# A DeltaNet mixer that keeps its keys unnormalised, with the z and gate projections merged and the layer norm's sums added over channel groups first

## The reference, cut to what matters

```python
qkv, z, b_logit, a_logit, cf_in = split(h @ w_in)          # 1536, 512, 4, 4, 1024 columns
q, k, v = split(silu(causal_conv4(qkv)))                   # 4 heads of 128
q, k = l2norm(q), l2norm(k)                                # x * rsqrt(sum(x*x) + EPS)
beta = sigmoid(b_logit);  g = -exp(a_log) * softplus(a_logit + dt_bias)
o = gated_delta_rule(q, k, v, g, beta)                     # S_t = e^g S + beta k (v - e^g S^T k)^T
o = rms_norm(o, dn_norm_w) * silu(z)
cf = silu(layer_norm(causal_conv31(glu(cf_in + b))))       # mean and variance over 512 channels
mixed = concat([o, cf]) @ w_out
```

## Time and profile before

| what | value |
|---|---|
| median of 3 runs | 2866.58 us (2862.74 to 2869.66) |
| the profiled execution's own time | 2864.63 us |
| its span, first to last instruction | 2862.8 us |
| mean granted clock of PE | 0.948 |
| PE busy, share of the span | 2533.9 us, 89% |
| DVE busy | 1337.9 us, 47% |
| ACT busy | 818.2 us, 29% |
| POOL busy | 477.5 us, 17% |

### The profile page before, as it was taken

The page is one execution under the profiler, slowest core; times in us unless marked ns, Lnnn a source line. Parts: engine busy times, 40 slices in busy tenths (PEclk is TensorE's granted clock), DMA queues, the critical chain, the costliest instruction groups (busy, mean ns, idle before and its releaser), DMA issues. The chain is left out here.

```text
span 2862.8 us, 48765 instructions
## 1 busy us (share of the span) xinstructions
PE 2533.9 (89%) x18064; PEld 1613.3 (56%) x18065; DVE 1337.9 (47%) x3734; ACT 818.2 (29%) x1760; POOL 477.5 (17%) x735
## 2 busy tenths in 40 slices
PE   6879999999999999999974699999999999999940
PEld 5567777887778877778852343334334343333310
DVE  1468787788887788887863200000000000000037
ACT  1213433343433343433331122222212122221211
POOL 0112221222221222212220210111101010100112
PEclk9889999999999999999976699999999999999975
DMA  9430000000000000000000899999999999999957
GB/s 357 167 121 16 32 24 24 32 32 16 32 17 31 32 22 25 32 17 31 24 24 25 341 376 398 401 387 427 385 398 399 367 427 376 423 420 410 365 230 315
DMA packets 84326, 570.79 MB, mean 199 GB/s; under 512 B 16189, under 2 KB 16573, under 8 KB 56138
## 3 DMA queue, kind: packets, MB, share of 16 engines
q1 hardware_dynamic: 67298, 525.47, 45.6%
q0 software_dynamic: 13824, 33.58, 3.0%
q10 hardware_dynamic: 3048, 9.34, 0.8%
HBM read 534.71 MB, written 50.40 MB: 204 GB/s over the span
## 5 line engine op out<-in xcount | busy, mean ns | idle before, releaser
L364 PE MATMUL pj_ps<-hT,win 128*128 128x128 f32 x5120 | 635.5, 279 | 4.4 <-issue 4.4
L364 PEld LDWEIGHTS pj_ps<-hT,win 128*128 128x128 f32 x5120 | 593.1, 192 | 23.0 <-issue 10.1
L1122 DVE SCALAR_TENSOR_TENSOR cvf<-cfpre,chp,cvf 128x128 f32<-128x128 f32 x1920 | 594.1, 372 | 12.6
L1802 PE MATMUL gate_ps<-longgu,xT 128*64 128x512 f32 x752 | 337.5, 602 | 31.3 <-DMA shortgu<-in_w_gate_dram 28.3
L1819 PE MATMUL y_ps<-longdn,hidT 128*64 128x512 f32 x752 | 331.4, 593 | 20.1 <-ACT hidT L1865 20.1
L1879 DVE TENSOR_TENSOR hid<-hid,up_ps 128x512 f32<-128x512 f32 x47 | 32.3, 688 | 670.4 <-PE up_ps L1802 670.4
L1802 PE MATMUL gate_ps<-shortgu,xT 128*64 128x512 f32 x752 | 337.5, 602 | 0.0
L1819 PE MATMUL y_ps<-shortdn,hidT 128*64 128x512 f32 x752 | 332.8, 595 | 0.0
L1802 PE MATMUL up_ps<-longgu,xT 128*64 128x512 f32 x752 | 330.4, 592 | 0.0
L1802 PE MATMUL up_ps<-shortgu,xT 128*64 128x512 f32 x752 | 330.4, 592 | 0.0
L1883 DVE COPY y<-y_ps 128x512 f32<-128x512 f32 x94 | 65.0, 692 | 381.2 <-PE y_ps L1819 381.2
(11 more groups left out here) (322 smaller groups left out, 3247.7 us busy)
## 6 DMA issues: line engine op xcount, KB each, us to landing
shortgu<-in_w_gate_dram SPq DMA_DIRECT2D x47, 2048.0 KB, 9.4
shortgu<-in_w_up_dram SPq DMA_DIRECT2D x47, 2048.0 KB, 13.7
shortdn<-in_w_down_dram SPq DMA_DIRECT2D x47, 2048.0 KB, 13.2
longgu<-in_w_gate_dram SPq DMA_DIRECT2D x20, 2048.0 KB, 13.4
longgu<-in_w_up_dram SPq DMA_DIRECT2D x20, 2048.0 KB, 18.1
longdn<-in_w_down_dram SPq DMA_DIRECT2D x20, 2048.0 KB, 18.9
wout<-in_w_ada_dram SPq DMA_DIRECT2D x12, 2048.0 KB, 8.7
yy<-y_dram SPq DMA_DIRECT2D x16, 1024.0 KB, 11.9
```

Of the source, the lines that this page charges most:

```text
L364: mm = pe.matmul(pj[bank][:, g % 4, :], t.win[:, k, col + (g % 4) * P:col + (g % 4 + 1) * P], hT[:, k, :], start=(k == 0), stop=(k == KD - 1))
L1122: ins = dve.scalar_tensor_tensor(cvf[:, g, :], src, w, cvf[:, g, :], ALU.mult, ALU.add)
L1802: mm = pe.matmul(out[sides[side], :], xT[:, k, sides[side]], w[:, m * KD + k, :], start=(k == 0), stop=(k == KD - 1))
```

## The change

Five edits go together.

1. The norms of the keys leave the keys. `scores` works on the raw keys (qkvT itself, channel-major), so khat, its transposes on PE and the evacuation of them on ACT disappear. ACT copies the key rows out of b5 (`krow`) and squares that copy. POOL makes rk = rsqrt(ssk1), sqk = ssk1 * rk (the norm), bk = beta * rk and bh = bk * rk; EU is multiplied by bh (in turn i, not at the end of the turn before). v is scaled by the norm (`scaled_values` on DVE, where `khats` was), and `state_values` subtracts in SBUF. The state update's key decay uses the last column of EU.
2. One of the three 4-column products of `decays` goes, and `front_kdb` on DVE.
3. z and the 8 gate columns (520 columns next to each other in w_in) become two products of 260 columns, in banks pj[0] and pj[1], on either side of `state_and_output`. `project_ba` goes. ACT evacuates with two Silu and a copy of 8 columns. z_evac is signalled after the three.
4. The sums of the layer norm over 4 channel groups: POOL adds the groups two and two, then one and one (`channel_sum`, `square_sum`), and PE multiplies one group with the ones matrix where it did four.
5. The query norm is folded in the head norm, so `head_rstd` has two steps where it had five, and POOL raises to a power once less.

```diff
@@ PE
-            def project_z(j, first, last):
+            def project_z(j, part):
-                if first == 0:
-                    pe.wait_ge(k_evac, j + 1)
-                for k in range(first, last):
-                    mm = pe.matmul(pj[0][:].rearrange("p a b -> p (a b)"), hT[:, k, :], t.win[:, k, COL_Z:COL_Z + DNW],
+                pe.wait_ge((k_evac, v_evac)[part], j + 1)
+                for k in range(KD):
+                    mm = pe.matmul(pjf[part][:, 0:ZH], hT[:, k, :], t.win[:, k, COL_Z + part * ZH:COL_Z + (part + 1) * ZH],
                                    start=(k == 0), stop=(k == KD - 1))
-                if last == KD:
+                if part == 1:
                     mm.then_inc(z_ps, 1)
...
-                pe.matmul(m_gate[:, 4:8], t.cst[:, C_LS, :], g4, start=True, stop=True)
-                pe.matmul(m_gate[:, 8:12], t.cst[:, C_ONE, :], g4, start=True, stop=True).then_inc(gates_ps, 1)
+                pe.matmul(m_gate[:, 4:8], t.cst[:, C_ONE, :], g4, start=True, stop=True).then_inc(gates_ps, 1)
...
             def ln_mean(i):
-                pe.wait_ge(cf_tap, CFT * (i + 1))
+                pe.wait_ge(csum_ready, i + 1)
                 pe.wait_ge(ssn_ready, i + 1)
-                for g in range(CFG):
-                    mm = pe.matmul(m_mean, t.cst[:, C_ONE, :], cvf[:, g, :], start=(g == 0), stop=(g == CFG - 1))
-                mm.then_inc(mean_ps, 1)
+                pe.matmul(m_mean, t.cst[:, C_ONE, :], csum, start=True, stop=True).then_inc(mean_ps, 1)
             def ln_var(i):
-                pe.wait_ge(xc_sq, i + 1)
-                for g in range(CFG):
-                    mm = pe.matmul(m_var, lnsq[:, g, :], t.cst[:, C_ONE, 0:1], start=(g == 0), stop=(g == CFG - 1))
-                mm.then_inc(var_ps, 1)
+                pe.wait_ge(vsum_ready, i + 1)
+                pe.matmul(m_var, lnsq[:, 0, :], t.cst[:, C_ONE, 0:1], start=True, stop=True).then_inc(var_ps, 1)
...
             def scores(i):
-                pe.wait_ge(khatT_ready, i + 1)
+                pe.wait_ge(k_copied, i + 1)
...
                 ada_turn(i, 8)
-                pe.wait_ge(khat_ready, i + 1)
-                for h in range(HEADS):
-                    mm = pe.transpose(b5[:, h, :], khat[:, h, :], ident)
-                mm.then_inc(khatT_ps, 1)
+                scores(i)
                 if front:
                     project(j, 4, 5)
-                scores(i)
...
                 if front:
-                    project_z(j, 0, KD // 2)
+                    project_z(j, 0)
                 state_and_output(i)
                 if front:
-                    project_z(j, KD // 2, KD)
-                    project_ba(j)
+                    project_z(j, 1)
@@ ACT
-                act.activation(zn[:], pj[0][:], ACT.Silu).then_inc(z_evac, 1)
+                act.wait_ge(ba_biased, j)
+                znf = zn[:].rearrange("p h c -> p (h c)")
+                act.activation(znf[:, 0:ZH], pjf[0][:, 0:ZH], ACT.Silu)
+                act.activation(znf[:, ZH:DNW], pjf[1][:, 0:DNW - ZH], ACT.Silu)
+                act.copy(bar, pjf[1][:, DNW - ZH:ZH]).then_inc(z_evac, 1)
...
             def key_squares(i):
                 act.wait_ge(kr_ps, i + 1)
+                act.wait_ge(dS_ps, i)
+                act.copy(krow[:], b5[:]).then_inc(k_copied, 1)
+                act.wait_ge(k_copied, i + 1)
                 act.wait_ge(ssk_eps, i)
                 for h in range(HEADS):
-                    ins = act.activation(tmp[:, h, :], b5[:, h, :], ACT.Square, accum_out=ssk[:, h:h + 1])
+                    ins = act.activation(tmp[:, h, :], krow[:, h, :], ACT.Square, accum_out=ssk[:, h:h + 1])
...
-                khat_evac(i)
@@ POOL
+            def key_norms(i):
                 pool.wait_ge(ssk_ready, i + 1)
...
+                pool.tensor_tensor(rk, ssk1, hp[:, 4:8], ALU.pow).then_inc(k_scale, 1)
+            def key_scales(i):
...
+                pool.tensor_tensor(sqk, ssk1, rk, ALU.mult).then_inc(sqk_ready, 1)
+                pool.tensor_tensor(bk, beta, rk, ALU.mult).then_inc(k_scale, 1)
+                pool.wait_ge(k_scale, 3 * i + 2)
+                pool.tensor_tensor(bh, bk, rk, ALU.mult).then_inc(k_scale, 1)
...
+                pool.tensor_tensor(EU[:], EU[:], over_cols(bh, P), ALU.mult).then_inc(EU_ready, 1)
             def key_decay(i):
...
+                pool.tensor_tensor(krow[:], krow[:], over_cols(EU[:, :, P - 1], P), ALU.mult).then_inc(kdec_ready, 1)
+            def channel_sum(i):
+                pool.wait_ge(cf_tap, CFT * (i + 1))
+                pool.wait_ge(qkv_act, i + 1)
+                pool.tensor_tensor(csum2, cvf[:, 0:2, :], cvf[:, 2:4, :], ALU.add).then_inc(csum_half, 1)
+                pool.wait_ge(csum_half, i + 1)
+                pool.tensor_tensor(csum, csum2[:, 0, :], csum2[:, 1, :], ALU.add).then_inc(csum_ready, 1)
+            def square_sum(i):
+                pool.wait_ge(xc_sq, i + 1)
+                pool.tensor_tensor(lnsq[:, 0:2, :], lnsq[:, 0:2, :], lnsq[:, 2:4, :], ALU.add).then_inc(vsum_half, 1)
+                pool.wait_ge(vsum_half, i + 1)
+                pool.tensor_tensor(lnsq[:, 0, :], lnsq[:, 0, :], lnsq[:, 1, :], ALU.add).then_inc(vsum_ready, 1)
...
             def turn(i, before, front, ahead):
                 j = i + 1
+                key_norms(i)
                 if before:
                     rsqrt_row(ss1, v1, rs1, mix_ss, mix_var, mix_rstd, i - 1)
-                keys(i)
+                key_scales(i)
                 if before:
                     rsqrt_row(ss2, v2, rs2, x1_ss, x1_var, x1_rstd, i - 1)
-                key_decay(i)
+                channel_sum(i)
                 mask(i, 0)
                 first_n(i)
                 mask(i, 1)
                 mask(i, 2)
                 state(i)
+                square_sum(i)
                 mask(i, 3)
                 ln_rstd(i)
+                key_decay(i)
@@ DVE
-            def khats(i):
-                dve.wait_ge(rqk_ready, 2 * i + 1)
-                dve.wait_ge(dS_ps, i)
-                dve.tensor_tensor(khat[:], b5, over_cols(rqk[:, 4:8], P), ALU.mult).then_inc(khat_ready, 1)
+            def scaled_values(i):
+                dve.wait_ge(sqk_ready, i + 1)
+                dve.wait_ge(vr_ps, i + 1)
+                dve.wait_ge(oa_ps, i)
+                dve.tensor_tensor(xv[:], b6, over_cols(sqk, P), ALU.mult).then_inc(vs_ready, 1)
...
-                dve.tensor_tensor(xv[:], b6, eS[:], ALU.subtract).then_inc(x_ready, 1)
+                dve.tensor_tensor(xv[:], xv[:], eS[:], ALU.subtract).then_inc(x_ready, 1)
```

More of the change, by code:

```diff
@@ L137, in build_mixer @@
         zn, zg = sb("zn", [P, HEADS, HD]), sb("zg", [P, HEADS, HD])
-        small = sb("small", [P, 96])
+        small = sb("small", [P, 104])
         qkvT = sb("qkvT", [P, QKVG, P])
@@ L155, in build_mixer @@
         P6 = KX
-        ssk, eps_k, ssk1 = ksum[:, 0:4], ksum[:, 4:8], ksum[:, 8:12]
+        ssk, eps_k, ssk1, rk, bk, bh, sqk = (ksum[:, 4 * n:4 * n + 4] for n in range(7))
         lnsq = sq[:, 0:CFG, :]
         lnd = cv[:, 2 * HEADS, :]
+        csum2, csum = cv[:, HEADS:HEADS + 2, :], cv[:, HEADS + 2, :]
         (ss0, rs0, ss1, rs1, ss2, rs2, v0, v1, v2) = (small[:, n:n + 1] for n in range(9))
-        ssn, rqk = small[:, 10:18], small[:, 18:26]
+        ssn = small[:, 10:14]
         bal, en, e8 = small[:, 26:34], small[:, 34:42], small[:, 42:50]
         l4, sp4, g4 = small[:, 50:54], small[:, 54:58], small[:, 58:62]
-        beta, kdb = small[:, 62:66], small[:, 66:70]
-        ex = small[:, 70:82]
+        beta, ex = small[:, 62:66], small[:, 70:78]
         oss, orr = small[:, 82:86], small[:, 86:90]
-        eps_d, eps_hd2 = small[:, 90:91], small[:, 91:95]
+        eps_d = small[:, 90:91]
+        bar = small[:, 96:104]
         hp = sb("half_pow", [P, 8])
-        scr = sb("scr", [P, 16])
+        scr = sb("scr", [P, 4])
         lnv, lnr = sb("ln_variance", [P, 1]), sb("ln_rstd", [P, 1])
@@ L216, in build_mixer @@
             "o_step", "o_ss", "o_rs", "o_gated", "oT_ps", "oT_ready"))
+        csum_half, csum_ready, vsum_half, vsum_ready = map(sem, (
+            "channel_sum_half", "channel_sum", "square_sum_half", "square_sum"))
         (mean_ps, xc_ready, xc_sq, var_ps, lnr_var, lnr_ready, lnd_ready, lnr_ps, cfn_ready, cf_ready) = map(sem, (
@@ L439, in scores @@
                 for h in range(HEADS):
-                    mm = pe.matmul(b7[:, h, :], khatT[:, h, :], qkvT[:, h, :], start=True, stop=True)
+                    mm = pe.matmul(b7[:, h, :], qkvT[:, HEADS + h, :], qkvT[:, h, :], start=True, stop=True)
                 mm.then_inc(attn_ps, 1)
@@ L445, in keys_on_state @@
                 for h in range(HEADS):
-                    mm = pe.matmul(b7[:, h, :], khatT[:, h, :], S[:, h, :], start=True, stop=True)
+                    mm = pe.matmul(b7[:, h, :], qkvT[:, HEADS + h, :], S[:, h, :], start=True, stop=True)
                 mm.then_inc(kS_ps, 1)
@@ L672, in _ @@
             ada(5)
```

(10 more changed lines are left out.)

95 lines of the change are left out of this document (34 added, 61 removed).

## The result

The changed kernel takes 2892.11 us (median of 4 runs, 2891.53 to 2894.28) against 2866.45 us of the kernel before: a ratio of 1.0091, 95% interval 1.0074 to 1.0109. It is slower by 26 us, where 2856 had been forecast, with 2838 to 2872 as the range: 20 us above its upper end.

The account below looks back on a forecast made before the run. The order of PE's work was taken to bound the mixer. Terms sum to -0.63 us a turn: -8.2 over thirteen turns, -1.6 in turn 14, -0.9 in turn 15, +0.1 in turn 0; -10.6 us, so 2856 us, range 2838 to 2872.

Parts of the forecast that it names:

- (a): z and gate products: PE's work falls 1.5 us, a new 1.0 us wait for ACT; turn 0.5 us shorter.
- (b): Keys to h2n: post begins 0.7 us later, and h2n comes 0.7 us later (bounds +0.3 and +1.7).
- (c): Layer norm mean on PE: eight instructions become two, 0.67 us less a turn.
- (d): Layer norm variance on PE: of eight instructions two stay, 0.66 us less a turn.
- (e): POOL's square_sum and mask 3 beside tap 0 on DVE, ahead of the first Q: +0.5 us a turn (bounds 0 and 1.2).
- Turn 0: First turn, where PE waits for DVE's convolution: POOL's sums laid bare, about +1.4 us; in all +0.1 us.
- (f): Parts said to cost nothing: scaled_values for khats, key_decay moved, head_rstd with three steps fewer, the khatT copy removed.
- Rival E: A 1.6 us wait before L576 brings PE's clock to 1.2 GHz for a while: 2868 to 2878 us; chance 0.04.
- Rival C: POOL's new sums hold DVE for their whole length: turn +1.0 us, in all +14 us, 2880 us; chance 0.16.

Follow-up runs that it names:

- b_z: The kernel before the change with only the z and gate columns made two products of 260 columns: 2858.6 us, ratio 0.9971.
- e_ord: a_pad3 with ACT squaring the mixed rows right behind its key-row copy and POOL making their norm ahead of the keys': 2844.66 us, ratio 0.9931.
- e_h2noln: e_ln with h2n made ahead of taps 29 and 30: 2839.55 us, ratio 0.9912.
- e_h2sq: a_pad3 with h2n made two taps earlier and POOL adding the squares ahead of the state's decay: 2823.59 us, ratio 0.9855.
- a_pad3: The changed kernel with three DVE no-ops right ahead of DVE's loop: 2860.46 us, ratio to the kernel before 0.9985.
- b_minus5: The kernel before the change with six mask copies made one instruction, 399 instead of 404 ahead of DVE's loop: 2890.53 us, ratio 1.0096.
- e_ln: a_pad3 with the layer norm's channel groups summed on PE again, POOL adding nothing: 2859.67 us, ratio 0.9986.
- b_h2: The kernel before the change with h2n made ahead of taps 29 and 30: 2856.19 us, ratio 0.9969.

## Why the prediction was wrong

**The steps, by the no-op version.** With code loading out of the way the kernel takes 2860 us, in the forecast range, and a turn without a fall of the clock 85.95 us: 0.70 less than 86.65, where the sum said 0.63. So each term can be held against its row.

- (a) z and gates: the wait was 0.90 us for 1.0; a product of 260 columns takes 3.51 / 16 = 0.219 us for the 0.221 of the straight line. `b_z` has the whole term at -0.41 for -0.5.
- (b) h2n (its sum nets -0.80 and +0.4 to -0.35, where it is -0.40, which changes nothing): from the start of `decays` to L566 it is 0.6 us later for 0.7. The parts are off in both directions. `post` came 0.9 us later for 0.7. EU times bh cost L1268 nothing for 0.4 (it still took 1.23 us and started on time), while the taps became quicker as said, 4.66 for 5.44 us. L1273 took 1.21 us for 0.75, 0.46 for 0.35. The order on POOL and ACT as a cause is shown by `e_ord`, where `post` comes 1.5 us earlier.
- (c), (d): 1.33 us of products, confirmed by the 1.27 us between `e_h2noln` and `e_h2sq`.
- (e): the wait for Q rose by 0.57 us for 0.5, and moving `square_sum` took just that back.
- Turn 0: the wait at the mean rose from 13.0 to 14.0 us, and is now put down to POOL, for the 1.4 us forecast.

**The step that failed** is in term (b): it lets `post` begin as soon as mix_rstd is there, at +0.7 us, and so PE wait some 1.6 us for h2n. Not even the list (f), "at nothing", names the removal of `front_kdb`, which is thus at nothing without a reason, and no term asked where the loop's code lies. The runs show in its place that DVE stands about 3.1 us at each of 12 jumps back until its code is there. That fell on the chain whose end PE already waited for: the wait for h2n is 2.89 us, not 1.6, the clock falls behind it, and a turn takes 89.04 us where the sum said 86.02. Of the signs that the prediction named for being wrong, the last one came: PE's clock in the loop is below 1.00.

**Rival E** was priced at 0.04. Its mechanism came true, its wait and its time did not: it spoke of a wait of 1.6 us and of 2868 to 2878 us. The argument against it was that waits of 1.24 us had left the clock at 1.00. A wait of 1.42 us (`a_pad3`) left it there too, and one of 2.05 us in `b_minus5`, but 2.89 us did not: the stretch behind it took 4.40 us for 2.78. These kernels also differ in PE's other waits (`b_minus5` has none before `front_transposes`), and no run changes the length of this wait alone. Rival C, slower through POOL's sums, had the right sign for the wrong reason: `e_ln` shows that these sums cost about what they give, no more.

The 26 us come out as: the sum of the five edits, -4 us by the ratio of `a_pad3` (with some turns at a lower clock in it, which the sum did not have and which hide some 6 of its 10.6 us); the jumps back, +30 us by the two ratios, of which 1.47 of each 3.09 us are PE's longer wait and 1.62 its slower work behind it.

The change also took packets off q8, 138 before and 30 after. By the three turns of `e_ln` they are PE's code. The kernel before fetches nine of them in every turn and the changed one none between 300 and 1390 us, and in the loop PE never stands at "issue" in either, so that this is no part of the 26 us.

## What to carry to other kernels

When an edit changes the number of instructions of an engine that has a long loop, look at the first instruction behind the jump back before believing any other explanation: idle time put down to "issue" there, and more packets on a queue of instructions, is code being fetched, and a few no-ops ahead of the loop tell within one run. A saving on the busiest engine is worth only what the next late chain leaves of it; here three small moves of work off that chain (h2n ahead of two taps, the square sum into POOL's idle time, the evacuation of z behind other products) were worth 53 us by the medians (2860.46 to 2807.07), against 4 for the change itself. Partial sums on a helper engine should be placed where it and its neighbour both have time.

## What the runs showed of the hardware

- The start of a loop one instruction earlier or later in DVE's program is worth some 30 us here: 402 ahead of it 2892.1 us, 403 ahead 2858.5 us in one run, 405 ahead 2860.5 us in ten runs. Five instructions fewer in the set-up make a tuned kernel 0.96% slower.
- What a stop for code costs on DVE: the first instruction comes 2.7 to 3.0 us behind the branch for 0.2 to 0.3, and the one behind the next border 2.3 to 2.7 us later again. On PE, in three turns of `e_ln`, the whole of it was 0.5 to 0.8 us a turn.
- An idle time of 0.27 us between two groups of PE cost 0.54, start to start (the kernel before against `b_h2`).
- PE's clock after a wait: 1.00 behind 2.05 us of waiting (`b_minus5`), 0.61 over 4.4 us behind 2.89 us (the changed kernel, in nearly every turn), and in four turns lower around a wait of 1.81 us (`a_pad3`, 0.87 in the 10 us that hold the wait and what follows), which left it at 1.00 in the other turns and in all of `e_ord`.
- A DVE instruction of 0.75 us beside POOL's first channel sum of 0.76 us takes 1.21 us. One of 1.23 us that begins 0.12 us ahead of the end of POOL's 1.04 us instruction is not held up.
